# A recurrent head on one core: other PSUM banks for the v transposes and the sample diagonal, k^T v products and state recurrence one tick later

## The reference

```
q, f, i, g = split(xn @ w_in)
log_f = logaddexp(log(lb), log1p(-lb) + log_sigmoid(f));  k = (1 - lb) * sigmoid(-f);  v = i
G = cumsum(log_f) within a chunk
A[t, s] = sum_d q[t,d] k[s,d] exp(G[t,d] - G[s,d])   for s <= t in the chunk
o = A v + (q exp(G)) S
S = exp(G_last) S + (k exp(G_last - G))^T v
o = rms_norm(o, norm_g) * silu(g);   output = o @ w_out
```

## Time and profile before

| | us |
|---|---|
| median of three timed runs | 1488.95 |
| lowest and highest of them | 1488.82, 1490.62 |
| the profiled execution: span from first to last instruction | 1489.4 |
| TensorE busy | 1409.5 (95%) |
| VectorE busy | 868.8 (58%) |
| ScalarE busy | 557.0 (37%) |
| GpSimd busy | 318.5 (21%) |

### The profile page before, as it was taken

How to read it: one execution, slowest core, us unless ns; L and a number is a source line. 1 busy time by engine, 2 the same in 40 slices (tenths; PEclk the granted TensorE clock), 3 DMA queues, 4 the chain that set the end, 5 groups by cost and what they waited for, 6 DMA issues and landing times.

```text
span 1489.4 us, 27801 instructions
## 1 busy us (share of the span) xinstructions
PE 1409.5 (95%) x10712; PEld 1373.8 (92%) x10712; DVE 868.8 (58%) x1319; ACT 557.0 (37%) x1022; POOL 318.5 (21%) x405
## 2 busy tenths in 40 slices
PE   8899998999999999978999999989799999999995
PEld 8887897999999999978999988889799999999995
DVE  6356538665656522278777878864766556553224
ACT  5234334433333322235444444433443333332221
POOL 2123224111111100143222222221511111111002
PEclk9989998999999999999999999989899999999998
DMA  7311121322222322221222222222122232233211
GB/s 261 90 44 55 58 86 39 89 84 87 95 85 84 117 97 79 76 70 57 73 86 86 73 70 75 70 73 87 44 75 95 87 96 85 84 111 110 78 39 60
DMA packets 38527, 123.33 MB, mean 83 GB/s; under 512 B 4104, under 2 KB 9864, under 8 KB 38344
## 3 DMA queue, kind: packets, MB, share of 16 engines
q1 hardware_dynamic: 31888, 110.74, 23.3%
q10 hardware_dynamic: 6408, 11.38, 2.0%
q0 software_dynamic: 176, 0.44, 0.1%
HBM read 113.98 MB, written 8.57 MB: 82 GB/s over the span
## 4 chain that ended last, share of the span: by engine, by line
PE 76%; DVE 15%; issue 4%; ACT 3%; ACTq 1%; DMA 0%; DVEq 0%; POOL 0%; SPq 0%
PE acc L365 68%; PE aux L577 2%; DVE w_lo L1039 2%; DVE x L1240 2%; PE aux L614 1%; DVE lev L1337 1%; DVE mix L1235 1%; PE acc L383 1%; DVE v_s L1492 1%; DVE scratch L1443 1%; DVE h_lo L1047 1%; DVE lev L1331 1%; PE aux L488 1%; DVE c_E L1494 1%; PE aux L468 1%
## 5 line engine op out<-in xcount | busy, mean ns | idle before, releaser
L1039 DVE TENSOR_TENSOR w_lo<-raw,w_hi 128x512 fp32r<-128x512 f32 (+1 forms) x372 | 320.6, 864 | 400.9 <-ACT w_hi L696 400.1
L365 PE MATMUL acc<-h_hi,w_hi 128*128 128x272 f32 x2208 | 477.4, 298 | 27.7 <-DVE h_lo L1047 22.9
L365 PE MATMUL acc<-h_hi,w_lo 128*128 128x272 f32 x2208 | 465.9, 293 | 0.0
L365 PE MATMUL acc<-h_lo,w_hi 128*128 128x272 f32 x2208 | 465.4, 293 | 0.0
L696 ACT CAST w_hi<-raw 128x512 fp32r<-128x512 f32 (+1 forms) x372 | 238.4, 643 | 425.4 <-PE acc L365 412.0
L365 PEld LDWEIGHTS acc<-h_hi,w_hi 128*128 128x128 f32 x2208 | 356.0, 193 | 37.7 <-issue 17.2
L365 PEld LDWEIGHTS acc<-h_lo,w_hi 128*128 128x128 f32 x2208 | 356.8, 194 | 0.0
L365 PEld LDWEIGHTS acc<-h_hi,w_lo 128*128 128x128 f32 x2208 | 354.7, 194 | 0.0
L365 PE MATMUL acc<-g_hi,w_lo 128*128 128x272 f32 x684 | 141.6, 288 | 0.0
L365 PE MATMUL acc<-g_hi,w_hi 128*128 128x272 f32 x684 | 141.4, 288 | 0.0
L365 PE MATMUL acc<-g_lo,w_hi 128*128 128x272 f32 x684 | 141.0, 288 | 0.0
(11 more groups left out here) (244 smaller groups left out, 1669.4 us busy)
## 6 DMA issues: line engine op xcount, KB each, us to landing
raw<-in_w_up SPq DMA_DIRECT2D x88, 512.0 KB, 3.5
raw<-in_w_down SPq DMA_DIRECT2D x32, 704.0 KB, 4.0
raw<-in_w_in_c SPq DMA_DIRECT2D x32, 512.0 KB, 3.5
raw<-in_w_in_ab SPq DMA_DIRECT2D x18, 512.0 KB, 3.6
raw<-in_w_out_ab SPq DMA_DIRECT2D x8, 512.0 KB, 3.6
S<-in_state ACTq DMA_DIRECT2D x8, 512.0 KB, 4.2
o_ss<-Snew ACTq DMA_DIRECT2D x8, 512.0 KB, 2.6
raw<-in_w_out_c SPq DMA_DIRECT2D x8, 512.0 KB, 3.5
```

The costliest lines, as they stand in the source:

```text
L365: mm = pe.matmul(acc[out][:, t, 0:H], w[slot][:, cols], mv[:, kk_, t * H:(t + 1) * H], start=start and k == 0 and q == 0, stop=stop and k ...
L1039: dve.tensor_tensor(w_lo[n % 2][:, to], raw[n % 4][:, cols], w_hi[n % 2][:, to], ALU.subtract).then_inc(lo_ready, 1)
```

## The change

On TensorE the v transposes go to the banks `A[3]` and `A[2]` and wait for `og_ready` instead of `kdT_copied`. The four k^T v products leave tick 7 and stand in the next head's tick 0, behind level 0 and the sample diagonal, now into `A[0]`. The sample diagonal goes to `A[3]` and waits for `v_hi` instead of `st_ready`; `st_ready` is waited for at tick 2, since level 3 writes `A[0]`. On VectorE the state recurrence goes from tick 7 to the end of tick 0 of the following head and reads `A[0]`; only its wait for the stores of the head before stays at tick 7. ScalarE reads the v transposes from the new banks.

```diff
@@ TensorE, hgrn_tick @@
                     if t == 0:
                         pe.wait_ge(C["diag_ready"], 2 * prev + 2)
+                        pe.wait_ge(C["kdT_copied"], prev + 1)
+                        levels(prev, 0)
                         pe.wait_ge(C["v_hi"], prev + 1)
-                        levels(prev, 0)
-                        pe.wait_ge(C["st_ready"], prev + 1)
-                        pe.matmul(A[2][0:NB * TS, 0:NB * TS], E2[:, TP:T], E1[:, TP:T], start=True, stop=True
+                        pe.matmul(A[3][0:NB * TS, 0:NB * TS], E2[:, TP:T], E1[:, TP:T], start=True, stop=True
                                   ).then_inc(C["al_done"], 1)
+                        for c in range(NCH):
+                            mm = pe.matmul(A[0][:, c * P:(c + 1) * P], kt[:, c, :], vt[:, c, :], start=True, stop=True)
+                        mm.then_inc(C["u_done"], 1)
...
                     if t == 2:
+                        pe.wait_ge(C["st_ready"], prev + 1)
                         levels(prev, 3)
                         levels(prev, 4)
...
                     if t == 6:
                         pe.wait_ge(evac, tile("in_c", 2) + 4 * cur)
-                        pe.wait_ge(C["kdT_copied"], cur + 1)
-                        for c in range(NCH):
-                            pe.transpose(A[0][:, c * P:(c + 1) * P], vv[:, c * CH:(c + 1) * CH], ident[:])
-                        pe.transpose(A[1][0:NB * TS, 0:P], vv[:, TP:T], ident[:]).then_inc(C["vcT_done"], 1)
-                    if t == 7:
-                        pe.wait_ge(C["vcT_copied"], cur + 1)
                         if prev is not None:
                             pe.wait_ge(C["og_ready"], prev + 1)
                         for c in range(NCH):
-                            mm = pe.matmul(A[2][:, c * P:(c + 1) * P], kt[:, c, :], vt[:, c, :], start=True, stop=True)
-                        mm.then_inc(C["u_done"], 1)
+                            pe.transpose(A[3][:, c * P:(c + 1) * P], vv[:, c * CH:(c + 1) * CH], ident[:])
+                        pe.transpose(A[2][0:NB * TS, 0:P], vv[:, TP:T], ident[:]).then_inc(C["vcT_done"], 1)
@@ VectorE, states @@
-            def states(prev, cur):
-
-                dve.wait_ge(C["u_done"], cur + 1)
-                if prev is not None:
-                    dve.wait_ge(state_out, 32 * prev + 32)
-                step.mark(dve.tensor_copy(Sst[:, 0, :], A[2][:, 0:P]))
+            def states(prev):
+
+                dve.wait_ge(C["u_done"], prev + 1)
+                step.mark(dve.tensor_copy(Sst[:, 0, :], A[0][:, 0:P]))
...
@@ VectorE, hgrn_tick, tick 0 @@
-                        came(2, 5)
-                        dve.copy_predicated(AT_s[:], mask_s[:], A[2][0:NB * TS, 0:NB * TS]).then_inc(C["al_taken"], 1)
+                        came(3, 5)
+                        dve.copy_predicated(AT_s[:], mask_s[:], A[3][0:NB * TS, 0:NB * TS]).then_inc(C["al_taken"], 1)
+                        states(prev)
@@ VectorE, head @@
-                    if t == 7:
-                        states(prev, hd)
+                    if t == 7 and prev is not None:
+                        dve.wait_ge(state_out, 32 * prev + 32)
```

More of the change, by code:

```diff
@@ L994, in hgrn_tick @@
                         act.wait_ge(C["vcT_done"], cur + 1)
-                        act.copy(vt[:].rearrange("p a b -> p (a b)"), A[0][:])
-                        act.copy(vt_s[:], A[1][R0, 0:P]).then_inc(C["vcT_copied"], 1)
-                        step.mark(act.copy(v_hi_s[:], A[1][R0, 0:P]))
+                        act.copy(vt[:].rearrange("p a b -> p (a b)"), A[3][:])
+                        act.copy(vt_s[:], A[2][R0, 0:P]).then_inc(C["vcT_copied"], 1)
+                        step.mark(act.copy(v_hi_s[:], A[2][R0, 0:P]))
                         step.wait(act)
@@ L1348, in states @@
                                                   eG[:, (c + 1) * CH - 1:(c + 1) * CH],
-                                                  A[2][:, c * P:(c + 1) * P], ALU.mult, ALU.add)
+                                                  A[0][:, c * P:(c + 1) * P], ALU.mult, ALU.add)
                     if c < NCH - 1:
```

## The result

The changed kernel is slower by 0.3%. Six timed executions have a median of 1493.93 us (1492.29 to 1497.78), six of the kernel before, on the same chip, 1489.77 us (1488.82 to 1490.62). The ratio is 1.0031, with a 95% interval of 1.0021 to 1.0041. In a later series of executions it was 1.0032 (1.0021 to 1.0043). The forecast was 1486.9 us, with a range up to 1491.8, so it was wrong in sign and size.

A forecast was written before the change was run, and what follows sets the result against it. Each head was taken as a chain of TensorE to half 4, then VectorE to L1494. Savings 1.3 + 6 x 0.4 - 1.0 = 2.7 us, less 0.7 for the clock, made 1488.95 - 2.0 = 1486.9 us; range 1483.5 to 1491.8.

The forecast's parts named there:

- point 7: TensorE's clock: idle of 2.3 us at tick 0 makes drops likelier; half a drop charged, 0.7 us, ends -3 and +8.
- Point 1: TensorE's v transposes no longer wait for `kdT_copied`: 0.80 us of wait gone per head; the `og_ready` wait costs nothing.
- Point 2: Products leave tick 7, half 0 ends 2.29 us sooner, but TensorE then waits 2.3 us at tick 0 for VectorE's L1494.
- rival C: All 21.7 us of TensorE's waits in the recurrent stage go, giving 1469 us; chance 0.03.
- Point 3: Tick 0, first level-0 matmul to half 1: 2.26 us instead of 2.64; 0.4 us saved per head (0 to 0.6).
- Point 4: VectorE's state recurrence, moved behind L1422, does not delay the rescaling: cost 0, at most 0.5 us a head.
- Rival D: The recurrence, stalled beside GpSimd, delays the rescaling by 0.4 us, so nothing is gained: 1489 us; chance 0.15.
- Point 5: Head 0: transposes start 2.1 us sooner, half 1 at 703.6 against 704.9; 1.3 us saved (0.9 to 1.8).
- Point 6: Last head: TensorE waits 5.4 us for L1494, then runs at the half clock; 1.0 us lost (0.5 to 2.5).
- Rival A: Idle of 2.3 us at tick 0 lowers the clock for long in most heads: 3.7 us slower, 1492.6; chance 0.17.
- Rival B: The clock holds at tick 0, so an earlier drop goes too: 4.1 us saved, 1484.8 us; chance 0.2.

The follow-up runs named there:

- second profile: The changed kernel run again unchanged, for another profile: median 1493.79 us, ratio 1.0032 to the kernel before; the profiled execution took 1497.36 us.

## Why the prediction was wrong

By its own steps:

The step that failed is point 7, the clock. The points before it held or erred to the careful side.

Point 1 held: no wait before the v transposes but one of 1.8 us in head 0.

Point 2 held in kind and was short in size: the idle at tick 0 is 2.81 to 2.86 us, not 2.29, because halves 6, 7 and 0, now run without stops, end 2.7 us sooner and not 2.29. The wait released by the product into E2 takes the place of the first two waits. With it rival C falls, that all 21.7 us of waits go.

Point 3 had 2.26 us from level 0 to half 1 and 0.4 us saved per head. It is 2.18, because the sum took the duration of the level-0 records, 1.16 us, where the distance to the next start, 783.27 - 782.18 = 1.09, counts. The larger part came behind that. Half 1 to tick 1 took 872.55 - 869.19 = 3.36 us before and takes 787.45 - 784.36 = 3.09 now, and the matmuls of tick 1 take 1.89 us instead of 2.00: where TensorE had started tick 1 just behind VectorE's L1422, it lost 0.38 us, not 0.05. The saving is 40.10 - 39.25 = 0.85 us per head.

Point 4 held. In the changed kernel VectorE runs the recurrence right behind the sample diagonal and then still waits for TensorE's half 1 (its timeline):

```profile
785.53 0.27 DVE L1340 COPY Sst<-aux 128x128 f32<-128x128 f32 x1
785.84 1.11 DVE L1343 SCALAR_TENSOR_TENSOR Sst<-Sst,c_eG,aux 128x128 f32<-128x128 f32 x3
787.65 0.72 DVE L1401 TENSOR_TENSOR scratch<-acc,rstd 128x544 f32<-128x544 f32 x1 [0.69 <-PE acc L365]
```

Rival D falls with it.

Point 5 was short: the product into E2 ended at 700.5 us, not 701.4, and half 1 started at 702.76 (702.96 in the second profile), so 2.1 us sooner and not 1.3. (These starts are of rows not shown.)

Point 6 held: the last head's idle is 5.6 us (5.4 foretold), its level 0 is slow again, and from the start of its half 5 to tick 1 it takes 998.14 - 974.02 = 24.1 us against 997.03 - 973.50 = 23.5, so 0.6 us are lost where 1.0 (0.5 to 2.5) was foretold.

Point 7 is the step that failed, a term that I chose more than worked out: "I charge half a drop: 0.7 us". From the first level 0 of the loop to that of the last head, six heads, it took 989.62 - 743.55 = 246.1 us before, 990.16 - 741.40 = 248.8 in the first profile after and 995.31 - 742.15 = 253.2 in the second. (The starts 741.40, 990.16 and 995.31 are of level-0 rows that are not shown.) Six heads at the full clock are 240.6 us before and 235.5 after. So the edit took 5.1 us off this stretch, and the lower clock took 5.5 us before and 13.3 and 17.7 after: 8 to 12 us more, where 0.7 was charged. The net on this stretch is 2.7 and 7.1 us. On the whole span it is 1.1 and 6.2 us, which brackets the measured 4.2.

The step failed in its count. It expected "five or six" drops after the edit, "some of them in place of those at tick 3". The first profile has 8 and the second 10 (table above), and those at tick 3 were not replaced but rose from 3 to 5. Those at tick 0 rose from 1 to 3 and 5, some of them long: this part follows from the idle, since the extra matmuls took it away. Why there are more at tick 3 is not shown.

The bound written beside that term, "-3 and +8", held the first profile's 7.8 us and not the second's 12.2, and the range did not reach as far as this bound. The evidence for more was in the profile: behind both idles above 3 us the clock had fallen, behind those of 1.30 in one case of six, and an idle of 2.3 was put near the harmless end. Rival A (0.17) named the mechanism at tick 0: level 0, products and half 1 run slowly behind the gathered idle, in three heads of the first profile and six of the second. Its time of 1492.6, 1.3 us from the result, is in part luck. It had 6.4 us for the clock and 2.7 saved, where the runs show 8 to 12 and about 6.6 (5.1 on the stretch, 2.1 in head 0, less 0.6 in the last head), and it had nothing for tick 3. The Trainium skill ("TensorE: Matmul & The Clock Gate", section on HAM oscillation) describes a clock that falls again in each iteration because of a wait in each; the second profile agrees, with 2.8 us of idle in every head of the loop and level 0 or the products slow in six of seven, and the first agrees less, with three of the six heads that had this idle. The waits in the page's own case are longer, 3 to 5 us. Rival B's condition (the clock holds at tick 0) was made by filling, and gave 1486.0 and 1479.5 us, on either side of its 1484.8.

What is shown: that filling the idle gives 8 to 14 us back, that it takes away the drops behind tick 0, and that the products at tick 0 cost 0.88 us a head at the full clock. What stays open: why the drops behind tick 3 come in six heads of one execution and in one or two of another with the same work there, and why the change made them more frequent. The last head's own share, 1.2 us by the traces, was too small to show in the times.

## What to carry to other kernels

When a wait on TensorE goes, ask which chain sets the next start; if that is another engine's, the waits are gathered into one longer idle, and the lower clock behind it has to be priced in every iteration. The stated range should reach as far as the bounds of that price. Work that can lie beside the other engine's chain belongs there and not behind it: with the recurrence moved, products beside VectorE's part of the chain gave 1475.3 us, products behind it 1493.9. A few matmuls without use, put ahead of the wait, tell whether an idle costs its clock. Look in the trace whether they fit into the idle, as those of the last head did not, and time more than one execution.

## What was not expected

The kernel with 5 extra matmuls per head was faster than that with 11 (1479.5 against 1486.0 us), although it leaves 1.7 us idle and the other 0.4. The kernel with 11 had three of ten executions at 1480.8 us and the one with 5 had five of six between 1477.9 and 1480.9, so the two kernels may differ only in how often an execution falls into the lower group of times; from so few this is not shown. In the profile of the kernel with 11, drops behind tick 3 come head after head at a distance of 40.8 us (821.97, 862.74, 903.52, 944.30 above), and the changed kernel too has heads of 40.8 us one after another. A drop can thus recur at the same place of each head, so that the count of drops in one profile says little about the mean.
